# Gate/up products in two halves of the weights, the second projection of the prior expert chunk by chunk between and behind them

## The reference, cut to what matters

```
gu = xb @ w_gate_up[e] + b_gate_up[e]
g = jnp.minimum(gu[:, :D_FF], SWIGLU_LIMIT)
u = jnp.clip(gu[:, D_FF:], -SWIGLU_LIMIT, SWIGLU_LIMIT)
act = (u + 1) * g * jax.nn.sigmoid(SWIGLU_ALPHA * g)
return act @ w_down[e] + b_down[e]
```

## Time and profile before

| what | value |
|---|---|
| median of 3 runs | 1727.53 us (1723.46 to 1727.85) |
| the profiled execution, its own time | 1725.22 us |
| its span in the profile | 1723.5 us |
| mean granted TensorE clock | 0.905 |
| PE busy | 1471.9 us, 85% of the span |
| DVE, ACT, POOL busy | 773.2, 355.5, 96.5 us |
| HBM read, written | 589.36 MB, 25.87 MB |
| gate/up loads, median from issue to landing | 15.7 us (126 of 2048 KB) |
| down loads, median from issue to landing | 18.2 us (64 of 2048 KB) |
| chain that ended last | PE 41%, DMA 20%; L1517 25%, gate/up loads 16%, L1554 8%, L1536 4% |

### The profile page before, as it was taken

The page is one execution under the profiler, slowest core; times in us unless marked ns, Lnnn a source line. Parts: engine busy times, 40 slices in busy tenths (PEclk is TensorE's granted clock), DMA queues, the critical chain, the costliest instruction groups (busy, mean ns, idle before and its releaser), DMA issues.

```text
span 1723.5 us, 32057 instructions
## 1 busy us (share of the span) xinstructions
PE 1471.9 (85%) x11950; PEld 591.5 (34%) x11951; DVE 773.2 (45%) x1120; ACT 355.5 (21%) x822; POOL 96.5 (6%) x173
## 2 busy tenths in 40 slices
PE   3878886778887969899998998898999899999970
PEld 2433333345433344332332332332332232332320
DVE  2789878987886244131232132132132131131326
ACT  3212212222222111121212122112122121121220
POOL 0000011000000000000000000000000000000000
PEclk8989995679898858999999998999999999998995
DMA  9557888989998685598999999999999999999986
GB/s 328 183 189 243 296 285 275 359 296 307 313 296 287 233 338 212 228 428 339 424 423 399 417 429 379 411 427 394 402 430 412 398 427 400 410 428 385 429 367 254
DMA packets 127292, 598.10 MB, mean 347 GB/s; under 512 B 20503, under 2 KB 20517, under 8 KB 102026
## 3 DMA queue, kind: packets, MB, share of 16 engines
q1 hardware_dynamic: 109088, 560.20, 82.3%
q10 hardware_dynamic: 8634, 20.00, 3.4%
q0 software_dynamic: 9504, 17.06, 2.6%
HBM read 589.36 MB, written 25.87 MB: 357 GB/s over the span
## 4 chain that ended last, share of the span: by engine, by line
PE 41%; DMA 20%; issue 1%; SPq 0%; DVE 0%; ACT 0%; ACTq 0%; DVEq 0%
PE pair L1517 25%; DMA wts<-in_w_gate_up 16%; PE bank L1554 8%; PE bank L1536 4%; DMA wts<-in_w_down 3%; DMA wts<-y_rows 1%; PE bank L1507 1%; PE bank L1624 1%; PE bank L1565 1%; PE bank L1605 0%; DVE v_ring L2148 0%; DMA h_tok<-h_rows,v_tok 0%; ACT k_T L1161 0%; SPq L646 0%; SPq L657 0%
## 5 line engine op out<-in xcount | busy, mean ns | idle before, releaser
L1517 PE MATMUL pair<-wts,h_T 128*32 128x512 f32 x4032 | 443.9, 597 | 9.6 <-DMA wts<-in_w_gate_up 5.0
L2070 DVE TENSOR_SCALAR q_T<-pair 128x512 f32<-128x512 f32 x32 | 22.1, 692 | 638.9 <-PE pair L1517 638.9
L1517 PEld LDWEIGHTS pair<-wts,h_T 128*32 128x32 f32 x4032 | 129.6, 111 | 307.9 <-issue 297.1
L1554 PE MATMUL bank<-wts,k_T 128*32 128x512 f32 x2048 | 228.3, 596 | 6.4 <-issue 4.9
L1536 PE MATMUL bank<-wts,h_T 128*32 128x512 f32 x992 | 133.1, 676 | 54.4 <-DMA wts<-in_w_gate_up 52.6
L1664 DVE TENSOR_TENSOR wts<-wts,q_b 128x1024 f32<-128x1024 f32 x128 | 158.0, 1234 | 23.3 <-DMA wts<-in_cache_k 17.6
L1667 DVE TENSOR_REDUCE sc<-wts 128x16 f32<-128x1024 f32 x128 | 156.2, 1220 | 4.4
L1151 ACT ACTIVATE h_T<-bank 128x512 f32<-128x512 f32 x66 | 35.9, 595 | 575.8 <-PE bank L1507 575.8
L1554 PEld LDWEIGHTS bank<-wts,k_T 128*32 128x32 f32 x2048 | 65.9, 110 | 146.3 <-issue 137.8
L1229 PE MATMUL pair<-wts,h_T 128*8 128x128 f32 (+1 forms) x480 | 96.0, 476 | 12.1 <-ACT h_T L860 6.4
L1161 ACT ACTIVATE k_T<-bank 32x256 f32<-32x256 f32 x256 | 95.7, 374 | 13.6 <-PE bank L1554 10.2
(11 more groups left out here) (333 smaller groups left out, 1411.0 us busy)
## 6 DMA issues: line engine op xcount, KB each, us to landing
wts<-in_w_gate_up SPq DMA_DIRECT2D x126, 2048.0 KB, 15.7
wts<-in_w_down SPq DMA_DIRECT2D x64, 2048.0 KB, 18.2
wts<-in_cache_k SPq DMA_DIRECT2D x256, 256.0 KB, 3.8
v_ring<-in_cache_v SPq DMA_DIRECT2D x160, 256.0 KB, 3.8
wts<-in_cache_v SPq DMA_DIRECT2D x96, 256.0 KB, 3.9
wts<-in_w_in SPq DMA_DIRECT2D x5, 2048.0 KB, 24.1
wts<-y_rows SPq DMA_DIRECT2D x4, 2048.0 KB, 15.1
wts<-in_w_out ACTq DMA_DIRECT2D x8, 512.0 KB, 6.6
```

What stands on the lines that cost most here:

```text
L1517: m = nc.tensor.matmul(PS[part][p0:p0 + 32, :], lhs[:, 32 * b:32 * b + 32], rhs[:, part * F + half * 512:part * F + half * 512 + 512], sta ...
L1554: m = nc.tensor.matmul(PS[4][p0:p0 + 32, :], act_T[0][:, k, a0:a0 + 32], chunk[c][:, k, n * 512:(n + 1) * 512], start=(c == 0 and k == 0), ...
```

## The change

In PE's block the gate/up products of an expert are made in two halves: back and front with chunks 0 and 1, then back and front with chunks 2 and 3 and the bias. Between the halves stand the products of the prior expert with its first down chunk, and behind the transposes of x those with its second. For an expert with over 96 tokens, the products of b = 1 with both down chunks stand in the first of these places, ahead of b = 0. The waits for `at_copied`, `y_front` and `y_back`, which stood ahead of the whole second projection, stand ahead of its first part. The sizes of both experts are loaded to registers at the start of the block, and there are four places with branches on them where there were two. For expert 1 the wait for `late_slots_done` moves from behind the transposes of x to behind the first half.

SP's order becomes chunks 0, 1 of expert i, chunk 4 of expert i - 1, chunks 2, 3 of expert i, chunk 5 of expert i - 1. The loads before the loop (experts 0 and 1, the first of expert 2) keep their order. DVE, ACT and POOL are unchanged. Matmuls, loads and bytes are the same in number.

The diff, cut to its core:

```diff
-            def load_gate_up(i, e):
-                for c in range(4):
-                    sp.wait_ge(w_used[c], i)
-                    load_chunk(c, e)
-            def load_down(i, e):
-                for c in range(4, 6):
-                    sp.wait_ge(w_used[c], i)
-                    load_chunk(c, e)
+            def load_used(c, i, e):
+                sp.wait_ge(w_used[c], i)
+                load_chunk(c, e)
...
-                sp.wait_ge(w_used[c], 2)
-                load_chunk(c, e)
-            load_down(1, 1)
+                load_used(c, 2, e)
+            for c in range(4, 6):
+                load_used(c, 1, 1)
             with sp.Fori(3, E) as i:
-                load_gate_up(i, expert_at(i))
-                load_down(i - 1, expert_at(i - 1))
+                for c in range(2):
+                    load_used(c, i, expert_at(i))
+                load_used(4, i - 1, expert_at(i - 1))
+                for c in range(2, 4):
+                    load_used(c, i, expert_at(i))
+                load_used(5, i - 1, expert_at(i - 1))
...
-            def gate_up_front(i, chunk=gu_chunk):
+            def gate_up_front(i, half, chunk=gu_chunk):
...
-                for c in range(4):
+                for c in range(2 * half, 2 * half + 2):
                     pe.wait_ge(w_full[c], i * 16 + 16)
                     for k in range(2):
                         m = products(hg_T[:, 2 * c + k, :], chunk[c][:, k, :], c == 0 and k == 0, False)
                     m.then_inc(w_used[c], 1)
-                pe.wait_ge(sel_done, i + 1)
-                products(sel[0:96, :], b_split[0:96, :], False, True).then_inc(gu_done, 1)
-            def gate_up_back(i, b, chunk=gu_chunk):
+                if half:
+                    pe.wait_ge(sel_done, i + 1)
+                    products(sel[0:96, :], b_split[0:96, :], False, True).then_inc(gu_done, 1)
+            def gate_up_back(i, b, half, chunk=gu_chunk):
...
+            def down_front(i, c, chunk=dn_chunk, full=w_full[4:6], loads=0):
+                pe.wait_ge(full[c], i * 16 + 16 * (loads + 1))
+                for k in range(4):
+                    for n in range(2):
+                        for b in range(2):
+                            p0, a0 = 64 * n + 32 * b, 64 * c + 32 * b
+                            m = nc.tensor.matmul(PS[4][p0:p0 + 32, :], act_T[0][:, k, a0:a0 + 32],
+                                                 chunk[c][:, k, n * 512:(n + 1) * 512],
+                                                 start=(c == 0 and k == 0), stop=(c == 1 and k == 3))
+                m.then_inc(w_used[4 + c], 1)
+            def down_back(i, b, c, chunk=dn_chunk, full=w_full[4:6], loads=0):
+                pe.wait_ge(full[c], i * 16 + 16 * (loads + 1))
+                for k in range(4):
+                    a0 = 64 * b + 32 * c
+                    for q in range(4):
+                        nc.tensor.matmul(PS[5][32 * q:32 * q + 32, 256 * b:256 * (b + 1)],
+                                         act_T[1][:, k, a0:a0 + 32], chunk[c][:, k, q * 256:(q + 1) * 256],
+                                         start=(c == 0 and k == 0), stop=(c == 1 and k == 3))
+            def size_of(i):
+                return pe.value_load(n_tok[0:1, bass.ds(i, 1)], min_val=0, max_val=CAP)
+            def by_size(size, front, back):
                 with pe.If(size > 64):
+                    back(0)
                     with pe.If(size > 96):
+                        back(1)
+                front()
+            def gate_up(i, size, half, chunk=gu_chunk):
+                by_size(size, lambda: gate_up_front(i, half, chunk), lambda b: gate_up_back(i, b, half, chunk))
+            def down(i, size, c, chunk=dn_chunk, full=w_full[4:6], loads=0):
+                with pe.If(size > 64):
+                    if c == 0:
+                        with pe.If(size > 96):
+                            for q in range(2):
+                                down_back(i, 1, q, chunk, full, loads)
+                    down_back(i, 0, c, chunk, full, loads)
+                down_front(i, c, chunk, full, loads)
...
-            def expert_block(i, before=None, front=gate_up_front, back=gate_up_back):
+            def expert_block(i, before=None, chunk=gu_chunk):
+                size = size_of(i)
+                size_before = None if before is None else size_of(before)
                 after(pe, gclip_done, i * 2)
                 pe.wait_ge(xt_copied, i * 2 + 2)
-                size = by_size(front, back, i)
+                gate_up(i, size, 0, chunk)
+                if isinstance(i, int) and i == 1:
+                    pe.wait_ge(late_slots_done, 1)
+                if before is not None:
+                    down_ready(before, isinstance(i, int))
+                    down(before, size_before, 0)
+                gate_up(i, size, 1, chunk)
                 transpose_x(i + 1)
                 if isinstance(i, int) and i == 0:
                     enter_late()
-                if isinstance(i, int) and i == 1:
-                    pe.wait_ge(late_slots_done, 1)
                 if before is not None:
-                    down_block(before, isinstance(i, int))
+                    down(before, size_before, 1)
                 for part in range(2):
                     pe.wait_ge(xt_copied, i * 2 + (part + 3))
                     pe.wait_ge(act_done, i * 2 + (part + 1))
@@ -1626,12 +1626,11 @@
                     m.then_inc(at_full, 1)
                 return size
-            def down_block(i, first, front=down_front, back=down_back, size=None):
+            def down_ready(i, first):
                 pe.wait_ge(at_copied, i * 2 + 2)
                 if not first:
                     pe.wait_ge(y_front, i)
                     pe.wait_ge(y_back, i)
-                by_size(front, back, i, size)
...
-            down_block(E - 1, False, last_down_front, last_down_back)
+            size = size_of(E - 1)
+            down_ready(E - 1, False)
+            for c in range(2):
+                down(0, size, c, last_dn, last_full)
```

More of the change, by code:

```diff
@@ L648, in _ @@
                     e = expert_at(j + E)
-                    load_gate_up(j + E, e)
-                    load_down(j + E, e)
+                    for c in range(6):
+                        load_used(c, j + E, e)
             sp.wait_ge(y_scattered, (n + E) * 16)
@@ L1543, in gate_up_back @@
                         products(hg_T[:, 2 * c + k, :], chunk[c][:, k, :], c == 0 and k == 0, False)
[L1544 to L1576, removed]
-            def last_down_back(_i, b):
-                down_back(0, b, last_dn, last_full)
-            def late_down_front(i):
-                down_front(i, loads=-1)
-            def late_down_back(i, b):
-                down_back(i, b, loads=-1)
@@ L1587, in by_size @@
-            def by_size(front, back, i, size=None):
-                if size is None:
-                    size = pe.value_load(n_tok[0:1, bass.ds(i, 1)], min_val=0, max_val=CAP)
+                if half:
+                    pe.wait_ge(sel_done, i + 1)
+                    products(sel[0:96, :], b_split[0:96, :], False, True)
+            def down_front(i, c, chunk=dn_chunk, full=w_full[4:6], loads=0):
[8 more added lines that the diff above has]
+                m.then_inc(w_used[4 + c], 1)
@@ L1591, in by_size @@
+            def size_of(i):
+                return pe.value_load(n_tok[0:1, bass.ds(i, 1)], min_val=0, max_val=CAP)
+            def by_size(size, front, back):
                 with pe.If(size > 64):
-                    back(i, 0)
+                    back(0)
                     with pe.If(size > 96):
-                        back(i, 1)
-                front(i)
-                return size
+                        back(1)
+                front()
+            def gate_up(i, size, half, chunk=gu_chunk):
+                by_size(size, lambda: gate_up_front(i, half, chunk), lambda b: gate_up_back(i, b, half, chunk))
@@ L1643, in _ @@
             pe.wait_ge(meta_out, 2)
-            expert_block(1, 0, first_gate_up_front, first_gate_up_back)
+            expert_block(1, 0, first_gu)
             with pe.Fori(2, E) as i:
                 expert_block(i, i - 1)
-            down_block(E - 1, False, last_down_front, last_down_back)
+            size = size_of(E - 1)
+            down_ready(E - 1, False)
+            for c in range(2):
+                down(0, size, c, last_dn, last_full)
             pe.wait_ge(meta_out, 3)
@@ L1652, in _ @@
                     size = expert_block(j + E)
-                    down_block(j + E, False, late_down_front, late_down_back, size)
+                    down_ready(j + E, False)
+                    for c in range(2):
+                        down(j + E, size, c, loads=-1)
         @block.vector
```

## The result

| | before | after |
|---|---|---|
| median, four runs of each on one chip | 1725.49 us (1721.46 to 1727.85) | 1797.13 us (1796.63 to 1797.86) |
| span of the profiled execution | 1723.5 us | 1795.6 us |
| mean granted TensorE clock | 0.905 | 0.880 |

The ratio is 1.0419, 95% interval [1.0399, 1.0438]: the change costs 4.2%, 71.6 us. The prediction was 1724.9, with 1715 to 1738 as its range. It was wrong.

A forecast was written before the change was run, and what follows sets the result against it. It took the busier eight DMA engines as the bound, 64.0 us a pair of experts, unchanged. Early loads -5.0 and tail +2.4 gave -2.6 us, from 1727.53 to 1724.9 us; range 1715 to 1738.

The forecast's parts named there:

- Split of the gate/up products: PE's gate/up halves: one register load and two branches added a block, taken as 0, at most 1 us a block.
- D in two parts: Second projection split on PE: act waits of 1.3, 1.0 or 0.5 us, PE's pair of blocks 60.5 us, hidden below 64.0.
- the slack of 3.5 us a pair: Steady part: PE's 60.5 us a pair against the loads' 64.0, so the new act waits stay hidden.
- rival 2: Act waits in every block lower PE's clock and make PE the bound: 66.9 us a pair, 1763 us; chance 0.14.
- The bound of eight engines: Steady part: gathers and scatters load only half the DMA engines, which limit a pair of experts to 64.0 us.
- rival 1: Half-rate DMA holes are lost bandwidth; work evened over 16 engines gives 61.1 us a pair, 1688 us; chance 0.10.
- Loads reordered: SP's new load order: no load waits behind a later slot release in the steady part, 0 us a pair.
- Pauses, start and tail: Early load pauses and start: last load 5 us earlier; tail behind it 2.4 us later; sum -2.6 us.
- the forecast case: Whole kernel: loads stay the bound, 1724.9 us, own range 1720 to 1731, chance 0.60.
- The pause near 795: Early loads on the slow DMA half: 6.5 us lost behind the block with over 96 tokens, expected to go.
- the last D: Tail, final second-projection products on PE: expected to stand at about 1670 us if the forecast was right.

The follow-up runs named there:

- hoist: The changed kernel with both sizes for the next block loaded in one load ahead of the act wait: 1722.18 us, ratio 0.9991.
- Halves: The changed kernel with the second projection whole again behind the transposes of x and the loads in the old order: 1713.9 us, ratio 0.9931.
- halves and a third load: The kernel with only the gate/up products split, plus one extra unused register load of a size per block: 1716.0 us, ratio 0.9954.
- third load: The changed kernel with one more register load of a size in each block, its value unused: 1823.12 us, ratio 1.0563.
- scatter twice: The kernel with only the gate/up products split, with each scatter of output rows issued a second time: 1758.74 us, ratio 1.0207.
- hoist, old loads: The changed kernel with sizes loaded ahead of the act wait, but SP's old order of loads: 1732.04 us, ratio 1.0043.
- order only: The kernel before the change with SP's new order of loads alone, PE's order unchanged: 1893.26 us, ratio 1.0996.

## Why the prediction was wrong, point by point

**The step that failed is "Split of the gate/up products": "I take 0, bound above by 1 us a block".** It argued from the earlier trace rows that today's branches leave no gap. That row was read rightly, but it shows a PE whose next wait is far away. The very next step, "D in two parts", puts an act wait of 1 to 2 us directly ahead of those instructions. The sum priced the two effects apart, and only the instructions that were added. What the wait lays bare is all that stands behind it, the old ones too: the loop's branch, both loads, the branch on the size. With that went the slack of 3.5 us a pair: PE's pair is 68.3 us for the 60.5 of the forecast, over the 64.0 of the loads. Measured, in the pair shown: 1.49 and 1.75 us idle, 2.7 us a pair over "hoist". "Halves" and "halves and a third load" show the instructions without the wait, 0 to 2 us in the whole run; "hoist" the wait without most of the instructions, 0.2 to 0.3 us a block; "third load" 0.84 us a block for one more.

**The second failure is the argument against rival 2.** The rival had the right place, the right order of events (PE becomes the bound, its clock falls, the chain is of PE and DVE alone). Its threshold was 1.7 us a block, where the measured pairs give (64.05 - 61.33) / 2 = 1.4. It got 0.14, and 1763 us at worst. Against it I set that the window with waits of 0.92 and 2.96 us kept a clock of 1.00. In the kernel after it fell behind 1.16 and 0.89 at 1307.7, before the 1.49, while behind the same two waits in "hoist" it mostly did not. So neither the sum of the pieces nor the pieces of one block start tell when it falls, and how the clock decides stays open. What is shown is that it falls less often without the gaps (0.99 in "hoist" from 870 to 1570, 0.93 in the kernel after). Rival 2's price, 66.9 a pair, was the clock in each block, 6.4; measured, the clock takes 4.2 and the gaps, which it lacked, 2.7, which with PE's own 61.3 are the measured 68.3. Over its 13 pairs that would be (68.3 - 64.0) x 13 = 56, not 38. And the rival was priced for the steady part alone: measured are 45.2 in eleven pairs and 26.9 ahead of and behind them, where the block starts have the same gaps (2.10 us at 754.56, 1.88 at 1683.17).

**D in two parts** held: act waits 1.16, 0.89 and 0.39 for 1.3, 1.0 and 0.5, and a pair on PE of 61.33 for 60.5, measured in "hoist", 0.5 of the difference being the two gaps of 0.31 and 0.19. (The forecast's three waits sum to 2.8, not to the 2.7 that it added, and it counts 12.5 pairs for one rival and 13 for the other; neither changes the outcome.)

**The bound of eight engines** held: 63.9 and 64.05 us a pair in "halves" and "hoist" at a clock of 0.99, and "scatter twice" moved it by 2.5 us for 0.58 MB. With it rival 1 falls: no kernel whose loads bound it has settled at 61. The Trainium skill ("DMA: Bandwidth & Descriptors", The descriptor swizzle) assigns, in a transfer over 128 partitions, partitions 0 to 63 to eight of the engines, and the 2.5 us agree with it.

**Loads reordered** at 0 us was right for the order beside its PE, and "hoist, old loads" shows what it saves there, 10 us; "order only" shows 168 us lost where PE frees the slots otherwise.

**Pauses, start and tail** can be read in "hoist", where the forecast case came about. c0 lands at 829.12, 6.84 us behind the load before it, and at 864.28, 7.56 behind, d0 at 841.31, 6.45 behind. Over the 4.9 of the full rate that is 1.6 to 2.7 us each, a part of which may be a gather's; 1.3 and 1.5 were forecast for blocks 5 and 6. The pause near 795 of the earlier trace rows is gone, and the last D starts at 1668.30 for "about 1670". The last weight load lands 6.2 us earlier than before, for 5 forecast. The whole is 2.9 us under the kernel before of its chip, for 2.6, and neither can be told from no change. "Halves" gains 11 us with the pauses gone: of the prediction's sum that term was real.

## What to carry to other kernels

A wait that is added to an engine that is the bound can cost, beside its own length, that of the register loads and branches behind it, which the queue had read ahead until then, and the clock as well; look at what stands behind a new wait, and load the registers of the next round ahead of it. Keep enough products between a chain of other engines and the wait for it: "halves" keeps 7.0 us of them there, and its transposes wait for nothing. It splits the gate/up products and leaves the second projection whole in that place, and it is the version to keep, 1713.9 us against 1725.1 and 1797.1. On a queue that issues in order, the loads must stand in the order in which their slots are freed. What "halves" leaves is the 64 us of the eight engines; spreading the gathered rows over both halves of the partitions was not tried, nor anything against the 4.41 us of idle at the start.

## What the runs showed of the hardware that was not expected

- A register load from SBUF on PE's queue is 0.30 us by its row. One more behind the act wait costs 0.84 us a block ("third load"); where the queue can read ahead it costs 0 to 2 us in the whole run.
- Products behind a row of short idle pieces ran slow: 64 matmuls in 9.29 us for 7.07 at the full 2.4 GHz. The granted clock is 0.50 for the first 4.4 us of the 9.29, and half of those are the 2.2 us lost. It had fallen behind waits of 1.16 and 0.89 us, before the gap of 1.49. Twelve transposes in the gap, without a shorter block, brought 7.07 back and 53 us in the run.
- One load that stands too early in SP's queue cost 168 us, more than twice what the whole change did, though it moves no byte more.
